# A feed-forward down projection by Strassen's scheme in place of the plain product, on one Trainium2 core

## What is computed

```
h2 = rmsnorm(x, norm2_g)
x = x + (silu(h2 @ w_ffn_gate) * (h2 @ w_ffn_up)) @ w_ffn_down
return rmsnorm(x, final_g)
```

## Time and profile before

| | us |
|---|---|
| median of three runs | 692.49 |
| profiled execution, all of it | 694.38 |
| its span | 692.3 |
| TensorE busy | 674.2 |
| VectorE busy | 483.7 |
| ScalarE busy | 378.7 |
| GpSimd busy | 36.6 |

### The profile page before, as it was taken

How to read it: one execution, slowest core, us unless ns; L and a number is a source line. 1 busy time by engine, 2 the same in 40 slices (tenths; PEclk the granted TensorE clock), 3 DMA queues, 4 the chain that set the end, 5 groups by cost and what they waited for, 6 DMA issues and landing times.

```text
span 692.3 us, 10920 instructions
## 1 busy us (share of the span) xinstructions
PE 674.2 (97%) x4042; PEld 602.6 (87%) x4042; DVE 483.7 (70%) x781; ACT 378.7 (55%) x638; POOL 36.6 (5%) x42
## 2 busy tenths in 40 slices
PE   4999999999999999999999999999999999999996
PEld 3998888888888878888899999999999998888884
DVE  4595648788887886854789997777888763333346
ACT  6436668788777873232675555554455553322244
POOL 0000401101122200000000000000000000000000
PEclk9999999999999999999999999999999999999999
DMA  8224202222222317331272344444423213313103
GB/s 290 73 72 128 67 14 67 67 70 66 70 62 66 121 62 274 121 122 62 62 184 60 84 108 116 122 121 121 110 73 71 110 61 123 121 61 121 62 0 122
DMA packets 73694, 67.25 MB, mean 97 GB/s; under 512 B 5887, under 2 KB 64446, under 8 KB 73662
## 3 DMA queue, kind: packets, MB, share of 16 engines
q1 hardware_dynamic: 73646, 66.82, 31.3%
q10 hardware_dynamic: 16, 0.00, 0.0%
HBM read 64.72 MB, written 2.10 MB: 97 GB/s over the span
## 4 chain that ended last, share of the span: by engine, by line
PE 95%; DVE 1%; ACT 1%; DMA 1%; issue 0%; SPq 0%
PE ps L407 21%; PE ps L408 20%; PE ps L409 20%; PE ps L1710 10%; PE ps L1713 10%; PE ps L1712 10%; PE ps L1619 2%; DMA raw<-in_w_in_dram 1%; PE ps L1569 1%; PE ps L1566 1%; PE ps L1451 1%; DVE w_lo L312 1%; ACT w_hi L302 1%; PE ps L1531 0%; DVE f_lo L1104 0%
## 5 line engine op out<-in xcount | busy, mean ns | idle before, releaser
L407 PE MATMUL ps<-hT_hi,w_lo 128*128 128x512 f32 (+1 forms) x288 | 100.7, 350 | 1.8 <-DVE hT_lo L978 1.8
L408 PE MATMUL ps<-hT_lo,w_hi 128*128 128x512 f32 (+1 forms) x288 | 99.2, 345 | 0.0
L409 PE MATMUL ps<-hT_hi,w_hi 128*128 128x512 f32 (+1 forms) x288 | 99.1, 344 | 0.0
L1710 PE MATMUL ps<-f_hi,w_lo 128*128 128x256 f32 x320 | 90.7, 283 | 0.0
L1713 PE MATMUL ps<-f_hi,w_hi 128*128 128x256 f32 x320 | 90.6, 283 | 0.0
L1712 PE MATMUL ps<-f_lo,w_hi 128*128 128x256 f32 x320 | 90.6, 283 | 0.0
L312 DVE TENSOR_TENSOR w_lo<-raw,w_hi 128x1024 fp32r<-128x1024 f32 (+3 forms) x55 | 64.2, 1173 | 35.0 <-ACT w_hi L302 33.7
L302 ACT ACTIVATE w_hi<-raw 128x1024 fp32r<-128x1024 f32 (+3 forms) x55 | 53.6, 984 | 39.6 <-PE ps L409 36.5
L819 ACT ACTIVATE w_hi<-scr 128x1024 fp32r<-128x1024 f32 x50 | 51.9, 1056 | 37.8 <-PE ps L1713 33.4
L1240 DVE TENSOR_TENSOR w_lo<-raw,w_hi 128x1024 fp32r<-128x1024 f32 x22 | 27.0, 1225 | 63.4 <-ACT w_hi L806 63.4
L407 PE MATMUL ps<-w_hi,f_lo 128*128 128x512 f32 x180 | 70.0, 389 | 0.0
(11 more groups left out here) (195 smaller groups left out, 1503.4 us busy)
## 6 DMA issues: line engine op xcount, KB each, us to landing
raw<-in_w_in_dram SPq DMA_DIRECT2D x12, 1024.0 KB
raw<-in_w_ffn_down_dram SPq DMA_DIRECT2D x11, 1024.0 KB, 4.9
raw<-in_w_ffn_gate_dram SPq DMA_DIRECT2D x10, 512.0 KB, 5.1
raw<-in_w_ffn_up_dram SPq DMA_DIRECT2D x10, 512.0 KB, 5.0
scr<-in_w_ffn_gate_dram SPq DMA_DIRECT2D x10, 512.0 KB, 5.2
scr<-in_w_ffn_up_dram SPq DMA_DIRECT2D x10, 512.0 KB, 5.9
raw<-in_w_out_dram SPq DMA_DIRECT2D x4, 1024.0 KB
xt<-in_x_dram SPq DMA_DIRECT2D x4, 512.0 KB, 6.6
```

Source lines behind the costliest of these rows:

```text
L407: nc.tensor.matmul(dst, l_lo, r_hi, start=start, stop=False)
L408: nc.tensor.matmul(dst, l_hi, r_lo, start=False, stop=False)
L409: return nc.tensor.matmul(dst, l_hi, r_hi, start=False, stop=stop)
L1710: nc.tensor.matmul(dst, wl[:, k, :], x_hi[:, k, :], start=start and k == 0, stop=False, skip_group_check=True)
```

## The change

The down projection is cut in halves of tokens (256), of features (11 tiles) and of columns (512), and done by seven block products, m = 0 to 6, in place of eight. A product runs over its 11 tiles in six "granules": five of two tiles and one of one, 42 in all. Each takes a block of weights of 512 columns and a block of features of 256 tokens, and fills two banks of PSUM; some products go on in the banks of earlier ones (`DN_BANK`), and after each product VectorE adds or subtracts the two banks into `xt` (`to_rows`), seven times two additions in place of eight.

Four of the products take sums of feature blocks. VectorE makes them in place in `store` (`next_sum`), one granule at a time, a product ahead. The products take sums of weight blocks, too. They are made by transfers that add to what lies in SBUF: GpSimd issues them (`add_block`, `accum_op=ALU.add`), once the granule's weights have been split and the earlier transfer has landed. There are two such lots, each of six granules: the "chain" in `raw` and the end of `scr` (products 0, 1, 2 and 6, with three additions) and the "second" in `scr` (3, 4 and 5; one addition, and a fresh load). The plain loads, 18, are issued by SP.

```diff
+        DN_A12, DN_A22 = 5, 6
+        DN_BANK = (0, 2, 0, 2, 0, 4, 0)
+        def dn_source(m, g):
+            return dn_second(g) if m in (3, 4, 5) else dn_chain(g)
...
+            for g in range(DN_GRANULES):
+                if g < 4:
+                    sync.wait_ge(w_ready, st_count("fg"[g // 2], STEPS // 2 - 1, 0))
+                else:
+                    sync.wait_ge(act_ready, 3 * STEPS + 2)
+                sync.dma_start(dn_chain(g), down_block(0, 0, g)).then_inc(chain_in[g], 16)
+            for g in range(DN_GRANULES):
+                sync.wait_ge(w_ready, T_DN + dn_n(1, g) + 1)
+                sync.dma_start(dn_second(g), down_block(1, 1, g)).then_inc(second_in[g], 16)
+            for g in range(DN_GRANULES):
+                sync.wait_ge(w_ready, T_DN + dn_n(4, g) + 1)
+                sync.wait_ge(second_add[g], 16)
+                sync.dma_start(dn_second(g), down_block(1, 0, g)).then_inc(second_in[g], 16)
...
+            def add_block(m, r, c):
+                for g in range(DN_GRANULES):
+                    pool.wait_ge(w_ready, T_DN + dn_n(m, g) + 1)
+                    if m == 3:
+                        pool.wait_ge(second_in[g], 16)
+                        nc.gpsimd.dma_start(dn_second(g), down_block(r, c, g), accum_op=ALU.add).then_inc(second_add[g], 16)
+                    else:
+                        pool.wait_ge(chain_add[g] if m else chain_in[g], 16 * max(m, 1))
+                        nc.gpsimd.dma_start(dn_chain(g), down_block(r, c, g), accum_op=ALU.add).then_inc(chain_add[g], 16)
+            add_block(0, 0, 1)
+            add_block(1, 1, 1)
+            add_block(2, 1, 0)
+            add_block(3, 0, 1)
...
+            for n in range(2, 7 * DN_GRANULES):
+                m, g = divmod(n, DN_GRANULES)
                 down_lo(n)
                 act_lo(n)
+                if m < 4:
+                    next_sum(m, g)
+                if m and g == 4:
+                    to_rows(m - 1)
...
+            def next_sum(m, g):
...
+                nc.vector.scalar_tensor_tensor(dn_act(m + 1, g), first, -1.0, second, ALU.mult,
+                                               ALU.subtract).then_inc(s_made, 1)
+            def to_rows(m, rows=range(2)):
...
+                    nc.vector.tensor_tensor(part, part, ps[:, DN_BANK[m] + i, :], op).then_inc(res_done, 1)
...
             for t in range(NT):
-                for c in range(2):
-                    residual(t, c)
-                    gained(t, c)
+                gained(t, 1)
+            for t in range(NT):
+                if t >= 2:
+                    to_rows(6, (t - 2,))
+                gained(t, 0)
                 last_root(t)
                 last_scale(t)
...
+            for m in range(6):
+                if m == 0:
+                    pe.wait_ge(act_ready, 3 * STEPS - 1)
+                elif m == DN_A12:
+                    pe.wait_ge(act_ready, 3 * STEPS + 2)
+                elif m > 1:
+                    pe.wait_ge(res_done, 2 * (m - 1))
+                for g in range(DN_GRANULES):
+                    used(down(dn_n(m, g)))
+            pe.wait_ge(res_done, 10)
+            for g in range(2):
+                used(down(dn_n(6, g)))
+            for i in range(2):
+                for g in range(2, DN_GRANULES):
+                    last = down(dn_n(6, g), (i,))
+                last.then_inc(dn_done, 1)
```

More of the change, by code:

```diff
@@ L54 @@
 FT = FF // P
+HALF_FT = FT // 2
 EPS = 1e-6
@@ L502, in _, with down_block @@
                         load_blocks(par, m, j)
[L504 to L515, removed]
+            def down_block(r, c, g):
+                first = HALF_FT * r + 2 * g
+                return w_fd_v[:, first:first + dn_tiles(g), 512 * c:512 * c + 512]
+            for g in range(DN_GRANULES):
+                if g < 4:
+                    sync.wait_ge(w_ready, st_count("fg"[g // 2], STEPS // 2 - 1, 0))
[9 more added lines that the diff above has]
+                sync.dma_start(dn_second(g), down_block(1, 0, g)).then_inc(second_in[g], 16)
             for t in range(NT):
@@ new lines, in to_rows @@
+            def to_rows(m, rows=range(2)):
+                t0, c, op, count = ((0, 0, ALU.add, 0), (2, 1, ALU.subtract, 0), (0, 1, ALU.subtract, 0),
+                                    (0, 1, ALU.subtract, 6), (2, 1, ALU.subtract, 4), (0, 0, ALU.add, 2),
+                                    (2, 0, ALU.add, 0))[m]
+                if m < 6:
+                    dve.wait_ge(w_used, T_DN + dn_n(m + 1, 0))
+                if count:
+                    dve.wait_ge(res_done, count)
+                for i in rows:
+                    if m == 6:
+                        dve.wait_ge(dn_done, i + 1)
+                    part = xt[:, t0 + i, 512 * c:512 * c + 512]
+                    nc.vector.tensor_tensor(part, part, ps[:, DN_BANK[m] + i, :], op).then_inc(res_done, 1)
@@ L1772, in _ @@
                     step(j, par)
[L1774 to L1779, removed]
-                return last
[L1782 to L1786, removed]
@@ L1789, in _ @@
[L1789 to L1807, removed]
@@ L1809, in _, with down @@
[L1809 to L1815, removed]
+            def down(n, rows=range(2)):
+                m, g = divmod(n, DN_GRANULES)
+                pe.wait_ge(w_ready, T_DN + n + 1)
+                pe.wait_ge(act_split, n + 1)
+                for k in range(dn_tiles(g)):
+                    for i in rows:
+                        dst, tok, col = ps[:, DN_BANK[m] + i, :], slice(256 * k + P * i, 256 * k + P * i + P), (
+                            slice(512 * k, 512 * k + 512))
+                        first, end = m in (0, 1, DN_A12) and not g and not k, g == DN_GRANULES - 1
+                        nc.tensor.matmul(dst, f_lo[:, n % 8, tok], w_hi[:, n % 4, col], start=first, stop=False,
+                                         skip_group_check=True)
+                        nc.tensor.matmul(dst, f_hi[:, n % 8, tok], w_lo[:, n % 4, col], start=False, stop=False,
+                                         skip_group_check=True)
+                        last = nc.tensor.matmul(dst, f_hi[:, n % 8, tok], w_hi[:, n % 4, col], start=False, stop=end,
+                                                skip_group_check=True)
+                return last
```

154 lines of the change are left out of this document (94 added, 60 removed).

## The result

The changed kernel takes 683.98 us (median of four runs, 683.45 to 684.68) against 692.47 for the kernel before beside it: a ratio of 0.9876, 95% interval 0.9863 to 0.9888. That is 8.5 us less, where 10.6 were forecast. Five more runs of the same kernel, on another occasion, have a median of 684.61, ratio 0.9883 (0.9863 to 0.9903). The first median lies 0.02 us inside the forecast's range of 680 to 684, the second outside it.

The account below looks back on a forecast made before the run. The prediction took the down stage as bound by PE alone, with the tail in series: 692.3 - 14.96 (66 matmuls) + 3.4 (longer tail) + 1.0 (accumulating transfers) = 681.7 us. Forecast range 680 to 684; 8 in 10, 678.5 to 697.

Parts of the forecast that it names:

- The longer end: After the last matmul: normalisation queues behind VectorE's last split and blocks' chains run in series; tail grows by 3.4 us.
- T: End of granule 37 in the last product, with 42 matmuls, 9.52 us, left; the tail's times count from it.
- Rival 3: End of the kernel: the tail does not grow; 677.5 us, up to 680 in part; chance 0.07.
- VectorE at 95%: Products 1 to 3 of the down stage: VectorE's work of 14.2 us fits in a product's 14.96.
- rival 4: Products 1 to 3: VectorE binds, waits eat its lead; costs 2 to 4 us; chance 0.16 together with rival 2.
- The accumulating transfers: Down stage: 22 units of 512 KB, each guessed at 2.7 us, adding 1 us; ends 0 and 53 us.
- The tightest point is granule 24: Start of the fifth product: transfers summed up to there must be through, allowing about 2.7 us per accumulate.
- the cover: Down stage: VectorE has split a granule 5.1 us before PE wants it.
- the sign of 90%: Expected sign in the trace: VectorE 90% or more busy from 581 to 625.
- rival 2: Down stage: accumulates somewhat late, 2.8 to 3.1 us each; stall 2 to 9 us, 684 to 691; 0.16 with rival 4.
- The start: First granules of the down stage: two extra VectorE sums and granule 4's late-requested weights cost 0, at most 0.5 us.
- Rival 1: Third and fifth products: accumulates fall behind, slower kernel from 3.2 us per 512 KB; chance of slower 0.25.

Follow-up runs that it names:

- e5_tail_full: Changed kernel with the end's work reordered: right-half gain products and squares earlier, first two blocks' chains interleaved; 681.58 us, ratio 0.9833.
- e1_plain: Changed kernel with the accumulating transfers issued as plain loads and the weight sums left out, so the output is wrong; 680.72 us, ratio 0.9828.
- e9_balance: e8_one_lot with right-half gain products and squares spread over the sixth and seventh products, some left-half ones after granule 41; 677.46 us, ratio 0.9787.
- e3_late_order: Changed kernel with the second lot's plain loads one product later and the third product's accumulates issued after the fourth's; 681.71 us, ratio 0.9838.
- e8_one_lot: e7_early with GpSimd's third accumulates of the first lot waiting for the sixth product's granules, not the third's; 677.81 us, ratio 0.9787.
- e6_both: Changed kernel with the edits of e3_late_order and e5_tail_full together; 680.89 us, ratio 0.9826.
- e7_early: e6_both with the first lot's two last loads moved to slots free some 10 us earlier; 678.51 us, ratio 0.9790.

## Why the prediction was right or wrong

The bound was right: PE at 0.2267 us a matmul, and 66 of them gone. The changed kernel's 462 stand at the same distance.

*The longer end was right in cause and size.* Forecast 3.4, measured 3.28. The timeline of VectorE in the changed kernel answers to the earlier trace rows:

```profile
664.31 0.41 DVE L1321 TENSOR_TENSOR f_lo<-store,f_hi 128x256 fp32r<-128x256 f32 x1
664.64 3.09 DVE L1508 TENSOR_TENSOR scr<-xt,fin_g 128x512 f32<-128x512 f32 x5
667.65 0.15 DVE L1513 SCALAR_TENSOR_TENSOR mse<-ssq 128x1 f32<-128x1 f32 x1
...
668.91 0.49 DVE L1521 TENSOR_SCALAR xt<-scr,rstd 128x512 f32<-128x512 f32 x1
...
671.54 0.49 DVE L1521 TENSOR_SCALAR xt<-scr,rstd 128x512 f32<-128x512 f32 x1
...
674.67 0.49 DVE L1521 TENSOR_SCALAR xt<-scr,rstd 128x512 f32<-128x512 f32 x1
...
677.81 0.49 DVE L1521 TENSOR_SCALAR xt<-scr,rstd 128x512 f32<-128x512 f32 x1
```

T is 671.65 - 9.52 = 662.13. The gain products start at T + 2.5, as forecast, and the four scales at T + 6.8, 9.4, 12.5 and 15.7, where 6.9, 9.6, 12.8 and 15.9 stood. Both parts of the step are there, the queue up to T + 2.5 and the chains of the blocks one behind the other. e5_tail_full takes the whole term away again. Rival 3, that the end does not grow, is refuted.

*VectorE at 95%: right.* Forecast were 14.2 us of work in the 14.96 of a product. VectorE's timeline in the changed kernel, at granules 6 and 12, with VectorE busy all the time between:

```profile
576.43 1.22 DVE L1326 TENSOR_TENSOR w_lo<-raw,w_hi 128x1024 fp32r<-128x1024 f32 x1
...
590.60 1.21 DVE L1326 TENSOR_TENSOR w_lo<-raw,w_hi 128x1024 fp32r<-128x1024 f32 x1
```

That is 14.17. In the first four products this load caused no stall by itself (e1_plain, e9_balance), so rival 4 did not come about. But it is why a delay lasts: of the 3.35 us, 0.61 stand before granule 18, when the transfers had landed and VectorE was still catching up (17.00 of 17.00 us busy from 608 to 625).

*The accumulating transfers: the step that failed, in place and size.* The price of an accumulate (c, per 512 KB) was about right. It was guessed at twice a plain one, 2.7 us; it holds the transfer engines 1.87 times as long, and ScalarE's weight copies for granules 24 to 26 of the changed kernel, each waiting for its accumulate with hardly a load beside them (the next were issued from 625.16 on), show it in time:

```profile
621.78 1.06 ACT L900 ACTIVATE w_hi<-scr 128x1024 fp32r<-128x1024 f32 x1 [3.33 <-DMA scr<-in_w_ffn_down_dram]
...
624.28 1.06 ACT L900 ACTIVATE w_hi<-scr 128x1024 fp32r<-128x1024 f32 x1 [0.92 <-DMA scr<-in_w_ffn_down_dram]
...
626.83 1.06 ACT L900 ACTIVATE w_hi<-scr 128x1024 fp32r<-128x1024 f32 x1 [0.97 <-DMA scr<-in_w_ffn_down_dram]
```

They are 2.50 and 2.55 us apart, less than the 2.72 of a granule. What was wrong is "The tightest point is granule 24". I summed the transfers over four products and compared them with four products' time. Their deadlines are one product away, so the sum has to be made per product. Done so, the second product has six accumulates and six loads, one each per granule, 4.0 us by measurement (2.7 + 1.34 = 4.04 already by the prediction's own figures) against 2.72. From granule 12 on ScalarE waits for transfers, and at 15 PE stands. Nor was the cover the 5.1 us of the prediction. VectorE enters the stage only 0.7 us ahead of PE (by the prediction's own paragraph on the start: ready at 570.6, wanted at 571.3) and gains 0.8 a product; in the changed kernel it has finished granule 11 at 590.34, 2.2 us before PE asks at 592.58.

Measured were 3.0 us of stall outside granule 4, forecast was 1.0, and that 1.0 had no working behind it: by its formula, 22 x (c - 2.7), both 2.7 and the measured 2.5 cost nothing. The stall in all, 3.35, is over the 3 us at which the prediction called itself wrong, and VectorE, busy for only 10.37 of the 15 us from 593 to 608, missed the sign of 90%. What came is rival 2, at its lower end (2 to 9 us of stall, 684 to 691), without the c of 2.8 to 3.1 that it asked for; by the prediction's own terms (680.9 before any stall) its times should have read 683 to 690. So that the time still fell at the edge of the forecast's range is luck: the range had room for a stall of 3 us that the sum put at 1.

*The start: "cost 0, at most 0.5".* It was 0.31 us here and 0.31 to 0.75 in the variants with accumulates that ask for the load as late. The load for granule 4, issued at 565.41, came in time for ScalarE's copy at 571.72, some 6.3 us after and not 5.1, beside the first accumulates; ScalarE sat idle 4.8 us for it. e1_plain, without them, has no stall there.

*The issuing.* In the changed kernel GpSimd's 512 KB accumulates took 1.20 us each to issue, 1.35 at most, also while VectorE was busy without a break (578 to 593). The Trainium skill ("SBUF — State Buffer", "Who interferes with whom") infers that VectorE's two-input operations do not starve the writing of such transfers' descriptors; this trace agrees.

*The rate.* Accumulates came 2.5 us apart at best, and one with a load 4.0. The estimate of 1.2 us of rate per 512 KB and no stall, which the prediction worked out from the Trainium skill ("DMA: Bandwidth & Descriptors", "Anatomy of one DMA — SWDGE (gpsimd) path"), does not hold for accumulates; the measurement decides.

Rival 1 did not come about: with accumulates all but alone c was 2.5, under its limit of 3.2, and in e3_late_order, where the accumulates of the second and the fourth product have no loads beside them, PE stands nowhere behind granule 4.

## What to carry to other kernels

Where transfers have deadlines, add them up in the window between request and deadline, not over the stage; two lots that each fit can be late together, and the answer can be to shift one of them (e8_one_lot). When a last stage finishes its outputs in another order, write out each engine's queue from the last release on: work that used to run under the matmuls may stand behind them, and moving it forward is only free while its engine still has a lead (e6_both).

## What else the runs showed

An accumulating transfer from HBM into SBUF, rows of 2 KB, costs GpSimd 1.20 us to issue in the changed kernel, against 0.72 for a plain one of the same shape in e1_plain. In e3_late_order, where the last six are issued without a pause, single ones take up to 3.8 us.

The start of the kernel varies from execution to execution. The stage began at 565.82 in the profile before, at 563.56 and 563.62 in two of the changed kernel, at 566.21 in e3_late_order. In the windows of the kernel before and of the changed one, in this order, the first products are already apart:

```profile
13.00:15.40 2.40, 1.32 (x6) 1.35 (x7) 2.40 (x6) 2.40 (x7) 0.00 (x0) 1.00 0.47 108
15.40:17.80 2.40, 2.40 (x15) 2.40 (x15) 1.65 (x7) 1.97 (x6) 0.00 (x0) 1.00 0.84 312
```

```profile
13.00:15.40 2.40, 2.33 (x18) 2.36 (x19) 2.40 (x7) 2.40 (x7) 0.00 (x0) 1.00 0.87 223
15.40:17.80 2.40, 2.40 (x22) 2.40 (x21) 1.24 (x7) 1.97 (x4) 0.00 (x0) 1.00 0.51 194
```

The first weights landed about 1.0 us later (ScalarE's first copy at 10.09 against 9.08), and the first matmuls of 256 columns then stood 0.21 us apart where they stood 0.12 in the other, 15 of them in a window in place of 22, with the granted clock at 1.00 in both. The profiles fall into two groups. In the kernel before, e3_late_order, e5_tail_full and e7_early TensorE had been idle for 1.64, 0.95, 0.77 and 1.05 us just before the first of these matmuls, 13 to 19 of them then stood 0.21 us apart, and the down stage began at 565.57 to 566.21. In the other eight it had been idle for 0.33 to 0.62 us, 1 to 7 stood so far apart, and the stage began at 563.37 to 564.22. Why the spacing doubles is open. For comparisons of 2 us it means: measure from the first instruction of the stage in question, not from the span's start.
